# Two blocks of a transformer on one core: values and transposes of stage one placed later, and another order of the first chunks and loads

## The reference, cut to what matters

```python
def mixer_dilated(h, w_qkv, q_gain, k_gain, w_o, cos, sin):
    qkv = (h @ w_qkv).reshape(B, S, 3, N_DIL, N_HEADS, HEAD_DIM)       # 1024 -> 9216
    q = apply_partial_rope(rmsnorm(qkv[:, :, 0], q_gain[:, None, :]), cos, sin)
    k = apply_partial_rope(rmsnorm(qkv[:, :, 1], k_gain[:, None, :]), cos, sin)
    v = qkv[:, :, 2]
    for g, (window, dil) in enumerate(((128, 1), (512, 4), (2048, 16))):
        o, m, d = band_attention(q[:, g], k[:, g], v[:, g], dil, window)
    wgt = d * exp(m - max over g); wgt = wgt / wgt.sum(over g)
    return einsum('gsh,gshd->shd', wgt, o).reshape(B, S, 1024) @ w_o

def first_block(x, ...):
    for i in range(DEPTH):
        x = x + mixer(rmsnorm(x, attn_norm[i]), ...)
        x = x + conv_ffn(rmsnorm(x, ffn_norm[i]), ...)
```

## Time and profile before

| | |
|---|---|
| median of 3 runs | 1072.74 us (1072.71 to 1072.81) |
| the profiled execution | 1073.2 us, its span 1071.4 us |
| PE busy | 1060.5 us, 99% of the span |
| DVE, ACT, POOL busy | 81%, 64%, 32% |
| HBM read | 181.35 MB, 170 GB/s over the span |
| stage one | from 8 us to about 291 us, a pair every 32.1 us |

### The profile page before, as it was taken

How to read it: one execution, slowest core, us unless ns; L and a number is a source line. 1 busy time by engine, 2 the same in 40 slices (tenths; PEclk the granted TensorE clock), 3 DMA queues, 4 the chain that set the end, 5 groups by cost and what they waited for, 6 DMA issues and landing times.

```text
span 1071.4 us, 20926 instructions
## 1 busy us (share of the span) xinstructions
PE 1060.5 (99%) x7404; PEld 978.1 (91%) x7404; DVE 865.4 (81%) x1581; ACT 683.8 (64%) x1256; POOL 342.3 (32%) x368
## 2 busy tenths in 40 slices
PE   8999999999999999999999999999999999999998
PEld 7999999999989999999899899999998998999998
DVE  7666777767799888887776999888896769998886
ACT  6667666666666656566776765555686667665563
POOL 6122212122155333332210555333351005643331
PEclk9999999999999999999999999999999999999999
DMA  8644544446467556535454576555433436665641
GB/s 318 210 144 146 165 146 149 141 142 229 138 201 216 193 194 189 173 103 192 133 177 149 163 215 202 189 186 186 152 116 129 158 119 193 208 203 181 195 157 41
DMA packets 57828, 183.31 MB, mean 171 GB/s; under 512 B 6432, under 2 KB 9760, under 8 KB 57504
## 3 DMA queue, kind: packets, MB, share of 16 engines
q1 hardware_dynamic: 57184, 181.90, 52.9%
q10 hardware_dynamic: 576, 0.52, 0.1%
HBM read 181.35 MB, written 1.05 MB: 170 GB/s over the span
## 4 chain that ended last, share of the span: by engine, by line
PE 93%; DVE 6%; DMA 1%; issue 0%; SPq 0%; ACT 0%; DVEq 0%; ACTq 0%
PE ps L386 23%; PE ps L388 11%; PE ps L562 8%; PE ps L564 8%; PE ps L563 8%; PE ps L1577 6%; PE ps L1579 6%; PE ps L1578 6%; PE ps L1070 2%; PE ps L1071 2%; PE ps L1072 2%; DVE prob L933 1%; DVE w_lo L365 1%; DVE prob L928 1%; PE ps L691 1%; PE ps L735 1%
## 5 line engine op out<-in xcount | busy, mean ns | idle before, releaser
L365 DVE TENSOR_TENSOR w_lo<-w_raw,w_hi 128x1024 fp32r<-128x1024 f32 (+2 forms) x372 | 448.6, 1221 | 50.2 <-ACT w_hi L357 49.6
L357 ACT ACTIVATE w_hi<-w_raw 128x1024 fp32r<-128x1024 f32 (+2 forms) x372 | 356.1, 971 | 162.6 <-PE ps L388 131.0
L386 PE MATMUL ps<-xg,w_hi 128*128 128x512 f32 x1056 | 371.6, 396 | 0.0
L388 PE MATMUL ps<-xg,w_lo 128*128 128x256 f32 x1056 | 293.0, 278 | 0.0
L386 PEld LDWEIGHTS ps<-xg,w_hi 128*128 128x128 f32 x1056 | 198.1, 188 | 44.2
L562 PE MATMUL ps<-w_hi,xg 128*128 128x384 f32 (+1 forms) x576 | 200.7, 349 | 1.5 <-DVE w_lo L365 1.5
L388 PEld LDWEIGHTS ps<-xg,w_lo 128*128 128x128 f32 x1056 | 198.4, 188 | 0.2
L564 PE MATMUL ps<-w_hi,xg 128*128 128x384 f32 (+1 forms) x576 | 193.3, 336 | 0.0
L563 PE MATMUL ps<-w_lo,xg 128*128 128x384 f32 (+1 forms) x576 | 193.0, 335 | 0.0
L1699 POOL TENSOR_TENSOR prob_t<-prob_t,qkT 128x256 f32<-128x256 f32 x63 | 101.2, 1606 | 286.1 <-ACT prob_t L1622 286.1
L1577 PE MATMUL ps<-g_hi,w_hi 128*128 128x256 f32 x528 | 147.9, 280 | 0.0
(11 more groups left out here) (171 smaller groups left out, 1364.7 us busy)
## 6 DMA issues: line engine op xcount, KB each, us to landing
w_raw<-w_stream SPq DMA_DIRECT2D x228, 512.0 KB, 3.7
w_raw<-w_stream SPq DMA_DIRECT2D x140, 384.0 KB, 3.2
w_raw<-w_stream SPq DMA_DIRECT2D x4, 392.0 KB, 3.1
xT<-x_a SPq DMA_DIRECT2D x4, 256.0 KB, 6.3
con<-consts SPq DMA_DIRECT2D x1, 1024.0 KB, 6.4
xT<-x_t SPq DMA_DIRECT2D x4, 256.0 KB, 8.1
conv_taps<-taps SPq DMA_DIRECT2D x1, 1024.0 KB, 6.1
par<-params SPq DMA_DIRECT2D x1, 592.0 KB, 7.5
```

The lines of the kernel that those rows point to most:

```text
L357: nc.scalar.activation(w_hi[s][:, 0:w], w_raw[s][:, 0:w], ACT.Copy).then_inc(w_hi_done, 1)
L365: nc.vector.tensor_tensor(w_lo[s][:, 0:w], w_raw[s][:, 0:w], w_hi[s][:, 0:w].bitcast(F32), ALU.subtract).then_inc(w_lo_done, 1)
L386: nc.tensor.matmul(bank(b, 0, 2 * TOK), w_hi[s][:, k * P:(k + 1) * P], xg[:, k, :, :].rearrange("p h t -> p (h t)"), start=(k == 0), stop= ...
L388: last = nc.tensor.matmul(bank(b), w_lo[s][:, k * P:(k + 1) * P], xg_hi[:, k, :], start=False, stop=(k == KT - 1), skip_group_check=True)
```

## The change: what it does

1. **Transposes of probabilities a chunk later.** prob_t_a_pe stands after chunks 5 and 6 instead of 4 and 5, ACT's copy a chunk later too. In the last pair, whose attention lies in the output projection, the transposes move half an output chunk (12 matmuls) back.
2. **Values behind the next scores.** pv_a_pe of pair pr, which stood after chunk 6 of the pair that follows, stands after chunk 1 of the pair after that, directly behind the scores of pair pr + 1. Its result no longer goes to bank 7 but to columns 384 to 511 of the two banks in which the q unit of pair pr + 2 is being accumulated (pv_part; pairs 0 to 5, joint). Pairs 6 and 7 still use bank 7. The four matmuls of 256 columns become eight of 128, one set for each bank. `mix_hi` and `mix_lo` read the two banks (pv_read, mix_place), at ACT's and DVE's chunks 6 and 7, and the v unit's first chunk, which takes the same banks, now waits for `mix_lo` (olo). The scores no longer wait for it.
3. **The transposes of q** (qt_pe) stand after chunk 9 instead of 7 (10 in the first pair), ACT's copy of them at its chunk 10.
4. **The first two units interleaved.** The chunks of units 0 and 1 (q and k of the first pair) alternate, so each part of the input is used by two chunks in a row. The host lays the stream out accordingly. Unit 2 takes banks 6 and 7, so that nothing of it waits for the norms, and the first scores wait for its copy (ve).
5. **The start.** Chunk 0 comes in two halves issued by ACT, with a semaphore each (first_in, w_loaded[0]), and is split in halves (first_split_hi, first_split_lo). SP's order becomes: parameters (with the norm weights), input part 0, chunk 1, part 1, chunks 2 and 3, part 2, chunks 4 and 5, part 3. ACT and DVE split chunk 4 before the loop. WARM_UP goes from 20 to 12.
6. **Other loads later.** The mask (1024 KB) is loaded behind chunk 16 instead of 8, the input in its own token order `x_t` (4 x 256 KB) behind chunk 22 instead of 12, the MLP parameters (592 KB) behind chunk 96 instead of 10.
7. Four semaphores that nothing uses are no longer allocated.

The core of the diff:

```diff
-WARM_UP = 20
+WARM_UP = 12
@@ unit_bank
+        if st == 0 and u == 2:
+            return S_BANK + t
         return 2 * ((u + (st == 2)) % 2) + t
@@ unit_chunk_pe
         u, q = divmod(n, UCH)
+        if st == 0 and n < 2 * UCH:
+            q, u = divmod(n, 2)
...
-            if st == 0 and u >= 2:
+            if st == 0 and u > 2:
                 if (u - 2) % 3 < 2:
                     eng.wait_ge(a.nm, 2 * (2 * ((u - 2) // 3) + (u - 2) % 3 + 1))
+                    if (u - 2) % 3 == 0 and u - 2 >= joint_unit(0):
+                        eng.wait_ge(a.olo, (u - 2) // 3 - 1)
@@ pv_a_pe
-        for kt in range(2):
-            for h in range(2):
-                lo, hi = HD * h, HD * h + HD
-                nc.tensor.matmul(bank(PVA_BANK)[lo:hi, :].rearrange("p (q c) -> p q c", q=2), band[:, kt, lo:hi],
-                                 prob_t[:, h, 0:2, kt * P:(kt + 1) * P], start=(kt == 0), stop=False, skip_group_check=True)
+        for t in range(2):
+            for kt in range(2):
+                for h in range(2):
+                    lo, hi = HD * h, HD * h + HD
+                    nc.tensor.matmul(pv_part(pr, t)[lo:hi, :], band[:, kt, lo:hi], prob_t[:, h, t, kt * P:(kt + 1) * P],
+                                     start=(not joint(pr) and t == 0 and kt == 0), stop=False, skip_group_check=True)
@@ mix_a_act
         eng.wait_ge(a.pv, pr + 1)
+        if joint(pr):
+            unit_wait(eng, 0, joint_unit(pr), 1)
+            eng.wait_ge(a.nm, 4 * (pr + 2) + 2)
+        nc.scalar.activation(mix_place(mix_hi[:, pr, :]), pv_read(pr), ACT.Copy).then_inc(a.ohi, 1)
@@ att_a_pe
-            if o in (4, 5) and p > 0:
-                prob_t_a_pe(eng, p - 1, o - 4)
-            if o == 6 and p > 0:
+            if o == 1 and p > 1:
+                pv_a_pe(eng, p - 2)
+            if o in (5, 6) and p > 0:
+                prob_t_a_pe(eng, p - 1, o - 5)
+            if o == 7 and p == PAIRS_AB - 1:
                 pv_a_pe(eng, p - 1)
-            if o == 7:
+            if o == (9 if p > 0 else 10):
                 qt_pe(eng, p)
```

More of the change, by code:

```diff
@@ L250, in build @@
     con_in = sem("con_in")
+    first_in = sem("first_in")
+    first_hi = sem("first_hi")
+    first_lo = sem("first_lo")
     rest_in = sem("rest_in")
@@ L658, in score_a_pe @@
         eng.wait_ge(a.ke, pr + 1)
-        past(eng, a.olo, pr, 0, None)
+        if pr > 0 and not joint(pr - 1):
+            eng.wait_ge(a.olo, pr)
+        if pr == 0:
+            eng.wait_ge(a.ve, 2)
         def band(qt):
@@ L707, in pv_a_pe @@
                 o = TOK + c % 2 * CLASS
-                last = nc.tensor.matmul(bank(PVA_BANK, c * CLASS, CLASS)[lo:hi, :], cls[:, c, lo:hi],
+                last = nc.tensor.matmul(pv_part(pr, c // 2)[lo:hi, c % 2 * CLASS:(c % 2 + 1) * CLASS], cls[:, c, lo:hi],
                                         prob_t[:, h, c // 2, o:o + CLASS], start=False, stop=True, skip_group_check=True)
@@ L920, in mask_a_dve @@
         if pr == 0:
[L921 removed]
+            eng.wait_ge(rest_in, 16)
         else:
@@ L1115, in att_a_pe @@
             unit_chunk_pe(eng, 0, n)
-            if o == 3 and p == 0:
+            if o == 5 and p == 0:
                 cols_pe(eng, 0, 0)
@@ L1978, in _ @@
         def _(act):
+            for kk, landed in ((0, first_in), (1, w_loaded[0])):
+                part = slice(kk * UNIT, (kk + 1) * UNIT)
+                act.dma_start(w_raw[0][:, part], stream_d[0, :, part]).then_inc(landed, 16)
             nc.scalar.preload_act_table_set("natural_log_exp_and_others")
-            for q in range(UCH):
-                resid_act(act, 0, 2 * q)
-                resid_act(act, 0, 2 * q + 1)
-                split_hi(act, q)
+            for kk in range(2):
+                resid_act(act, 0, kk)
+                first_split_hi(act, kk)
+            split_hi(act, 1)
+            resid_act(act, 0, 2)
+            split_hi(act, 2)
+            resid_act(act, 0, 3)
+            split_hi(act, 3)
+            resid_act(act, 0, 4)
+            resid_act(act, 0, 5)
+            split_hi(act, 4)
+            resid_act(act, 0, 6)
+            resid_act(act, 0, 7)
             for m in range(X_SQ_POOL, KT):
@@ L2003, in _ @@
             dve.wait_ge(par_in, 16)
-            for q in range(UCH):
-                resid_dve_lo(dve, 0, 2 * q)
-                resid_dve_lo(dve, 0, 2 * q + 1)
-                if q < AHEAD:
-                    split_lo(dve, q)
+            for kk in range(2):
+                resid_dve_lo(dve, 0, kk)
+                first_split_lo(dve, kk)
+            split_lo(dve, 1)
+            resid_dve_lo(dve, 0, 2)
+            split_lo(dve, 2)
+            resid_dve_lo(dve, 0, 3)
+            split_lo(dve, 3)
+            resid_dve_lo(dve, 0, 4)
+            resid_dve_lo(dve, 0, 5)
+            split_lo(dve, 4)
+            resid_dve_lo(dve, 0, 6)
+            resid_dve_lo(dve, 0, 7)
             gains_dve(dve)
@@ L2075, in weight_stream @@
             unit([m[:, (r * NDIL + g) * D + pr * P:(r * NDIL + g) * D + (pr + 1) * P] for g in range(NDIL)])
+    chunks[0:2 * UCH] = [chunks[u * UCH + q] for q in range(UCH) for u in range(2)]
     outs(w["a_w_o"][0], OUT_ORDER[0])
```

117 lines of the change are left out of this document (81 added, 36 removed).

## The result

The changed kernel takes 1063.75 us in the median of 4 runs (1063.4 to 1064.01) against 1072.78 us (1072.71 to 1072.88, 4 runs) for the kernel before on the same chip. The ratio is 0.9916, with a 95% interval of 0.9904 to 0.9928: 9.0 us faster. The forecast was 1064.5 us.

The account below looks back on a forecast made before the run. PE, working in 99% of the span, was taken as the bound. Waits 6.2, values 0 and start 2.0 us sum to 8.2 us, giving a median of 1064.5 us; own range 1062.5 to 1066, with rivals 1061.8 to 1067.6.

Parts of the forecast that it names:

- The waits: PE's wait for DVE's division before the first half of the transposed probabilities, eight times: 6.2 us gone, bounds 4 to 6.3.
- The next-late chain: Chain from q's norm to `mix_lo`, ahead of the v unit's first chunk: 1.2 us to spare, so no wait.
- Rival 2: Wait moves to `mix_lo` before the v unit; 0.5 us late in six pairs returns 3 us, 1067.5 us; chance 0.07.
- The values: Value matmuls on PE: split loses 0.6 us, standing behind scores gains 0.6 us, so 0; upper bound 10.3 us lost.
- The rule on weight loads: Skill rule that same-row-group loads do not overlap matmuls: split values cost 3.4 us, sum 4.8 instead of 8.2 us.
- Rival 3: Narrower value matmuls' weight loads not hidden: up to 10.3 us, 1074.8 us; middle case 1066.8 us; chance 0.05, 0.03 slower.
- The start: PE's first chunks, fed by transfers, ACT and DVE, come earlier: 2.0 us gained; bounds 4.0 gained to 1 lost.
- The point foretold: Start of chunk 6 on PE between 21.5 and 22.5 us, against 23.9 us for the comparable point before.
- rival 1: Start gives nothing: extra weight transfers ahead of input part 1 delay the first chunks; 1066.5 us; chance 0.17.
- the layout: Step times laid out for the start: chunk 0 from 6.6 us, chunk 5 at 18.6 to 19.1, chunk 6 at 21.7 to 22.2.
- The later loads: Loads moved later take 2.6 MB out of the first 25 us; nothing counted for it.
- Rival 4: DVE shifts with PE, division stays late in all pairs but the last: 0.8 and 2.0 us left, 1069.9 us; chance 0.03.

Follow-up runs that it names:

- the start alone: Changed kernel with the stage's body put back in the old order, values still split: 1071.87 us against 1072.56 for the kernel before, ratio 0.9994.
- the first experiment: Kernel before with the transposes of probabilities a chunk later (half an output chunk in the last pair), values whole after chunk 7: 1065.39 us, ratio 0.9933.

## Why the prediction was right, point by point

**The waits: 6.2 us forecast, 6.76 in the body by the move alone.** The mechanism is shown: the wait goes with the move and comes back with the old order. The size was a little low in two ways. The count by start times, 0.79 us a wait, leaves out that PE restarts slower behind a wait. From the last chunk matmul to the third after the transposes, a pair with the wait takes 84.14 - 82.13 = 2.01 us and the half without it 86.90 - 85.73 = 1.17, so 0.84 us each. And 0.1 us was taken off for no row's sake. Seven pairs at 0.84 and the tail at 0.77 are 6.65 us. The last 0.1 us of the 6.76 was not traced further.

**The next-late chain** held. `mix_lo` ended at 117.31 us, and PE began the v unit at 118.28 without a wait: 1.0 us to spare, where 1.2 was forecast. Rival 2 is out. These rows of ACT and DVE answer to the last of the earlier trace rows:

```profile
114.74 0.64 ACT L878 ACTIVATE mix_hi<-ps 128x256 fp32r<-128x256 f32 x1
...
116.68 0.63 DVE L1017 TENSOR_TENSOR mix_lo<-ps,mix_hi 128x256 fp32r<-128x256 f32 x1
```

**The values: 0 forecast, 1.2 to 1.3 us gained.** This is the term that was mis-sized. The forecast set 0.6 us lost in the split against 0.6 us gained in the merging. The split costs 0.06 us in eight pairs, a tenth of the estimate: the fit to the narrow matmuls charged each instruction 0.010 us of its own, and two instructions of half the width go through nearly as fast as one. The merging gave 0.21 us a pair. The forecast's 0.1 us was right for each border, though no row stood beside it, but its sum went wrong: "on each side, six times" is twelve borders, 1.2 us, and it counted six. With both sides in it the forecast's pair would have had 0.2 us for the merging, as measured. A pair came to 31.05 us and not to 31.2 to 31.4.

**The rule on weight loads.** The loads are as long as in the earlier trace rows, 137 ns, and eight more a pair cost under 0.01 us. By the rule of "TensorE: Matmul & The Clock Gate" in the Trainium skill, the section on packing small matmuls, loads of one row group are not overlapped, and the estimate by that page's price of a column was 3.4 us. The runs do not bear it out for these fp32 matmuls: two kernels that differ in the split measured 247.00 and 247.06 us. Rival 3 is out.

**The start: 2.0 us forecast, 0.7 to 1.6 measured** (1.6 between the two profiled executions, 1.1 by the spans and 0.7 by the times of the start alone, 0.8 by the spans of the changed kernel and the first experiment, 2.0, less 1.2 of body). The point foretold, chunk 6 between 21.5 and 22.5 us, came at 22.32, so the frame was right, but its inner steps were not. Chunk 0 was laid out at 6.6 us and started at 7.38 to 7.9, because input part 0 landed at 5.26 us behind ACT's own transfers; that they share the DMA engines was said only in rival 1. The fall of the clock in the gap was in the bounds and not in the layout. Against that, the later transfers landed 1.1 to 1.4 us earlier than laid out (part 1 at 7.65 for 9.0, chunk 2 at 8.6 for 10.0). The end of the warm-up, laid out at 6.4 us, lay between 5.4 and 6.6 us in the five profiles with twelve matmuls. The errors partly cancel, so that chunk 6 came in its window is in part luck. With the gap closed, the wait of chunk 5 stands at 19.08 us, for which the layout had 18.6 to 19.1; taken away too, the start gives 0.8 us more. Rival 1, that the start gives nothing, stands against spans that are 1.1 us shorter, but the times of the start alone do not exclude it (interval across 1). Of the three terms this is the one least well known.

**The later loads: 0 forecast, 0 measured** (245.78 us of body with and without). Rival 4, that the division stays late because DVE shifts with PE, is out with the first experiment.

The sum as it came out: 6.76 for the waits and 1.22 for the rest of the body, all but the 0.06 of the split the merging's, and 1.6 for the start, 9.6 us of span in the profiled execution. The median moved by 9.0; of the 0.6 between them, the time around the span is the part that shows (2.2 and 1.8 us in the two profiled executions, 1.8 to 2.9 in the four runs of the changed kernel). The forecast of 8.2 was too low in the body by 1.8 us and too high in the rest by 1.0. That the total was nearer than its two parts is luck.

## What to carry to other kernels

Where PE is the bound, price a wait by the starts of the instructions around it, restart included, and not by the idle time shown. Where two edits give the same late operation more time, undo each alone: here either would have done in six pairs of eight, and what the second brought was something else, a run of small matmuls less. When PE's start is brought forward, lay out the transfers with all queues that issue at that time, see whether the warm-up reaches the first real matmul (here closing the gap moved the later marks by 0.2 us and the median span by 0.1), and look for the operation that is late next, here the weight split of chunk 5.

## What the runs showed that I had not expected

- A change between the chunks' 128*128 tiles and the scores' or values' smaller tiles costs PE 0.10 us on entering and 0.11 us on leaving; before fp32 transposes with full tiles it costs nothing on entering (0.17 us step). The rows show this for three tile shapes (64*128, 64*64, 128*64); whether the tile or the operands make the difference was not tried alone.
- After 2.0 us of idle time at the start the granted clock was 0.50 in the windows from 8 to 10 us, and back at 1.00 from 11. It does not follow each time: with the transposes put back, 2.1 us of idle time went ahead of the same fall, but in the three other profiles with 12 warm-up matmuls PE stood idle for 1.1, 1.5 and 1.5 us and the granted clock stayed at 1.00. By the mean granted clock (0.998 where it fell) it is 7 of the 27 runs with 12 matmuls and none with 18 or 20. With 18 warm-up matmuls and no such gap chunk 0 ran at 2.4 GHz from the second matmul on.
- Input part 1, issued at the same moment, landed after 4.1 us in one kernel and 5.9 us in another with the same start. A single profile's first 20 us are good to about 1 us. The Trainium skill, "DMA: Bandwidth & Descriptors", the section on issuing engines not being separate queues, says that transfers of all issuing engines run interleaved on the same 16 DMA engines. The runs agree: input part 0 took 2.8 us in the two kernels in which ACT issues nothing there, and 4.1 to 4.4 us in the eight in which it issues 384 KB.
- The time around the span is 1.8 to 1.9 us in all runs of the kernel before and of the three kernels with 18 warm-up matmuls (22 and 13 runs). With 12 it lies between 1.8 and 2.9, from run to run (27 runs of five kernels, 2.8 or more in 7 of them). It goes with the short warm-up; by what way stays open.
